# Two feed-forward blocks: one 512-column matmul for the high and low activation halves, and an evacuation in two parts

## The chip, the cores and the metric

The kernel runs on one core of one Trainium2 chip. The metric is the device time of one execution in microseconds; lower is better. The core has five engines with queues of their own: PE (TensorE, matmuls, with its weight loads shown as PEld), DVE (VectorE), ACT (ScalarE), POOL (GpSimd) and SP (SyncE, which here only issues DMAs). They meet through semaphores.

## The reference, cut to what matters

Two transformer-like blocks run one after the other on 256 tokens of width 1024, all in float32. Each ends in a feed-forward part of hidden width 2816, and only these two parts are touched:

```
# block 1 (conv_ffn), grid rows of 64 tokens
u, g = split(h @ up_w, 2)                 # (256,1024) @ (1024,5632)
g = g_left*w[0] + g*w[1] + g_right*w[2] + b   # within each row of 64 tokens
y = (silu(g) * u) @ down_w
# block 2
gate, up = split(hn @ w_gate_up, 2)
h = h + (silu(gate) * up) @ w_down
```

## The kernel before, in words

**Split precision.** Every large product is computed from halves. A weight or activation is rounded to `hi` (the engine's fp32r format), and `lo` is the remainder; the product is hi·hi + hi·lo + lo·hi, three matmuls (`mm3`, lines 1917 to 1922). Activations stand transposed (features on partitions, 256 tokens along the row) in `h_hi` and `h_lo`, each [128, 8, 256].

**Weights.** A weight group of 1 MB arrives by DMA in one of three slots of `raw`; ACT casts it to `w_hi` (`hi_ahead`, line 658), DVE subtracts to make `w_lo` (`lo_ahead`, line 1261), and PE then reads both. All three rings have three slots. ACT may cast group s once PE has used group s-3 (`group_used`); SP may load group s once DVE has finished group s-3 (`lo_ready`).

**Feature tiles.** In the stages `up` (22 groups) and `gate_up` (22 groups) one weight group is one tile: 8 slices k of 128 inputs by 256 output features, that is two runs f of 128 features. `feature_tiles` (line 1986) multiplies, for each f and k, three matmuls of 256 columns (tokens) each: 48 in a tile. One tile fills one PSUM bank of 512 columns (f = 0 in the first half, f = 1 in the second). The first tile in each pass of the loop takes another order (lines 1993 to 2009), 48 matmuls too, with waits for the activations.

**Pairs.** Tiles 2j and 2j+1 are a pair j (gate and up of the same features), 11 pairs, run as a hardware loop of three rounds of three pairs (u = 0, 1, 2) and two pairs behind it. `up` puts its pairs in banks (4,5), (0,1), (2,3), `gate_up` in (0,1), (2,3), (4,5). PE starts pair j once DVE has finished pair j-3 (`act_full`).

**Evacuation of `up`, pair j.** ACT (line 933): two Identity activations from PSUM (middle tap and bias) into `cv`, cast of weight group 2j+3, Silu of `cv`, cast of group 2j+4, cast of the product to `act_hi`. DVE (line 1604): four `scalar_tensor_tensor` (left and right tap, for each f) that read PSUM and add into `cv`, `w_lo` of group 2j+3, the product `cv` times the up tile from PSUM into `actf`, `w_lo` of group 2j+4, `act_lo`.

**Evacuation of `gate_up`, pair j.** ACT (line 1168): Silu straight from PSUM, the two weight casts, cast to `act2_hi`. DVE (line 1855): `w_lo` of group 2j+3, the product from PSUM, `w_lo` of 2j+4, `act2_lo`.

The `down` and `down2` products that follow use 512-column matmuls: the activations are the stationary operand and 512 weight columns move. `m_bcast` (line 2273) is the one fp32r matmul whose moving operand consists of two separate runs of 256 columns (`mw[:, :, d, :]`).

Of the kernel before, what the change touches and what calls it, by code (L numbers as in the profile page):

```python
# [14 lines left out]
F32R = mybir.dt.float32r  # L15
ALU = mybir.AluOpType
# [3 lines left out]
P = 128  # L20
# [31 lines left out]
NORM_BANKS = {"norm2": (6, 7, 2, 3), "norm3": (4, 5, 0, 1), "norm4": (4, 5, 6, 7),}  # L52
TOKEN_BANKS = (4, 5, 6, 3)
NEG = -1.0e30


def plan_groups(I):
# [74 lines left out]
def two_blocks(nc, I, out):  # L132
# [5 lines left out]
    with ExitStack() as ctx:  # L138
# [15 lines left out]
        }  # L154

        FAMILY["act_full"] = (("up", ROUND + PAIRS), ("gate_up", ROUND + PAIRS))
        for kind in ("conv_mid", "conv_done", "silu_ready", "act_hi_ready", "act_lo"):
# [23 lines left out]
        x = sb(ctx, "x", [P, TT, D])  # L181
        full = sb(ctx, "full", [P, KD, T])
        yg = full[:].rearrange("p k t -> p (k t)").rearrange("p (t n) -> p t n", t=TT)
        h_hi = sb(ctx, "h_hi", [P, KD, T], F32R)
        h_lo = sb(ctx, "h_lo", [P, KD, T], F32R)
        ident = sb(ctx, "ident", [P, P])
        s_le_t = sb(ctx, "s_le_t", [P, P])
        s_ge_t = sb(ctx, "s_ge_t", [P, P])
# [187 lines left out]

        def p_rows(n):
            return out[0, :, n * NB:(n + 1) * NB].rearrange("(t p) n -> p t n", p=P)

        def in_round(s, r):  # L380

# [263 lines left out]
        def _(act):  # L645
# [287 lines left out]
            def up_step(r, u):  # L933
                j = ROUND * r + u
                act.wait_ge(group_used, U0 + 2 * j + 1)
                act.wait_ge(S("act_full"), j + 1)
                for f in range(2):
                    k = 2 * j + f
                    act.activation(cv[:, u, f, :], ps[:, up_bank(u), f * T:(f + 1) * T], ACT.Identity,
                                   bias=pcol("conv_b", k), scale=pcol("conv_w", KF + k)).then_inc(S("conv_mid"), 1)  # L940
                hi_ahead(U0 + 3, r, u)
                act.wait_ge(S("conv_done"), 2 * j + 2)
                act.activation(cv[:, u], cv[:, u], ACT.Silu).then_inc(S("silu_ready"), 1)
                hi_ahead(U0 + 4, r, u)
                act.wait_ge(S("act_full"), ROUND + j + 1)
                act.copy(act_hi[:, bass.ds(2 * j, 2), :], actf[:, u]).then_inc(S("act_hi_ready"), 1)
# [280 lines left out]
        def _(dve):  # L1227
# [364 lines left out]

            post_norm("post1", "norm2", gp1, (2, 4), p_parts)
            dve.sem_inc(S("act_full"), ROUND)
            transposed("norm2", NORM_BANKS["norm2"], lambda k: mod2[:, KD + k:KD + k + 1], lambda k: mod2[:, k:k + 1])

            def half_of(bank):
# [5 lines left out]

            def up_step(r, u):
                j = ROUND * r + u
                for f in range(2):
                    k = 2 * j + f
                    dve.wait_ge(S("conv_mid"), 2 * j + 2)
# [5 lines left out]
                    dve.scalar_tensor_tensor(rows[:, :, :-1], src[:, :, 1:], pcol("conv_w", 2 * KF + k), rows[:, :, :-1],  # L1614
                                             ALU.mult, ALU.add).then_inc(S("conv_done"), 1)
                lo_ahead(U0 + 3, r, u)
                dve.wait_ge(S("silu_ready"), j + 1)
                dve.wait_ge(group_used, U0 + 2 * j + 2)
                dve.tensor_tensor(actf[:, u], cv[:, u], half_of(up_bank(u) + 1), ALU.mult).then_inc(S("act_full"), 1)
# [234 lines left out]

            def gate_up_step(r, u):
                j = ROUND * r + u
                lo_ahead(V0 + 3, r, u)
                dve.wait_ge(S("silu_ready"), PAIRS + j + 1)
                dve.wait_ge(group_used, V0 + 2 * j + 2)
                dve.tensor_tensor(actf2[:, u], sil[:, u], half_of(2 * u + 1), ALU.mult).then_inc(S("act_full"), 1)  # L1860
# [55 lines left out]
        def _(pe):  # L1916
# [69 lines left out]
            def feature_tiles(s, bank, r=0, ready=None, between=None):  # L1986


                s, r = in_round(s, r)
                pe.wait_ge(lo_ready, s + 1 + 2 * ROUND * r)  # L1990
                hi, lo = part_view(w_hi, s), part_view(w_lo, s)
                if ready is not None:
                    for f in range(2):
                        fs_ = slice(f * P, (f + 1) * P)
                        for k in range(KD):
                            if f == 0:
                                pe.wait_ge(S("hi"), base("hi", ready) + k + 1)
# [12 lines left out]
                for f in range(2):  # L2010
                    if f == 1 and between is not None:
                        between()
                    fs_ = slice(f * P, (f + 1) * P)
                    for k in range(KD):
                        ins = mm3(ps[:, bank, f * T:(f + 1) * T], (hi[:, k, fs_], lo[:, k, fs_]),
                                  (h_hi[:, k, :], h_lo[:, k, :]), k == 0, k == KD - 1)
                ins.then_inc(group_used, 1)

            def tile_turned(t):
# [351 lines left out]
            def ffn(name, norm, bank):  # L2371

                def step(r, u):
                    pe.wait_ge(S("act_full"), base("act_full", name) + ROUND * r + u + 1)
                    if name == "up" and u == 1:
                        pe.wait_ge(S("p_out"), TT)
                    for half in range(2):
                        feature_tiles(at[name][2 * u + half], bank(u) + half, r, norm if u == half == 0 else None)

                rounds(pe, step)  # L2380

            def second(name, first, hi, lo, banks, gate=None, middle=None, tail_groups=2):

                pe.wait_ge(S("act_full"), base("act_full", first) + PAIRS + ROUND - 2)
# [8 lines left out]
                gate_vector(3, 0)  # L2393

            transposed("norm2", lambda: p_product(0))
            ffn("up", "norm2", up_bank)
            second("down", "up", act_hi, act_lo, (2, 6), gate=gate2, tail_groups=3)


# [296 lines left out]
                att_out(2, t)  # L2696
                att_out(3, t)
            transposed("norm4")
            ffn("gate_up", "norm4", lambda u: 2 * u)
# [36 lines left out]
```

## Time and profile before

| what | value |
|---|---|
| median of 3 runs | 824.05 us (822.19 to 825.15) |
| profiled execution, its time | 822.81 us |
| its span | 821.0 us |
| PE busy share of the span | 96% |
| DVE / ACT busy share | 62% / 48% |
| granted PE clock, mean | 0.993 of full |

The span is the time from the first to the last instruction in the profile; the execution's own time is 1.8 us longer. The matmuls overlap each other, so a matmul's duration is a latency; how fast they follow each other is read from the start times.

### The profile page before, as it was taken

Reading aid. Unit: us, or ns where it says so; the run is one execution under the profiler, and the core shown is the slowest. Engines: PE = TensorE matmul, PEld = TensorE weight load, DVE = VectorE, ACT = ScalarE, POOL = GpSimd, SP = SyncE. Lnnn points to the kernel's source line nnn. Section 1 sums busy time; section 2 is a strip of 40 time slices with the busy share of each in tenths; the row PEclk is TensorE's granted clock in tenths of the full one; section 3 lists DMA queues with packets and bytes.
Section 4 is the critical chain, followed back from the end, with each engine's and each line's share of the span. In section 5 each row is a group of like instructions: output and inputs, shape, how many; then the busy total and the mean of one; then the engine's idle time right before and its main releaser. Section 6 shows DMA issues by size and latency. Waiting matters only on the chain. (4 is left out here: it accounts for less than half of the span.)

```text
span 821.0 us, 12736 instructions
## 1 busy us (share of the span) xinstructions
PE 786.1 (96%) x5175; PEld 701.5 (85%) x5175; DVE 511.3 (62%) x670; ACT 390.3 (48%) x538; POOL 92.7 (11%) x150
## 2 busy tenths in 40 slices
PE   4898999999999999999989999999999999999996
PEld 3677777777799999988789988988799999998884
DVE  1664789866685766667477785664464545454465
ACT  2623413444675565544366555456364443433264
POOL 4000221301100000000070313210100000000000
PEclk9999999999999999999999999999999999999998
DMA  9973577733276545569536342321465555546611
GB/s 308 361 242 132 200 265 263 263 103 127 92 231 205 165 163 185 203 226 317 175 95 192 103 154 75 110 75 58 148 229 165 195 187 170 191 145 203 221 62 52
DMA packets 107901, 144.85 MB, mean 176 GB/s; under 512 B 6343, under 2 KB 70352, under 8 KB 107856
## 3 DMA queue, kind: packets, MB, share of 16 engines
q1 hardware_dynamic: 100512, 137.38, 50.3%
q10 hardware_dynamic: 7280, 6.83, 2.7%
q8 instruction: 32, 0.52, 0.3%
q14 instruction: 13, 0.11, 0.0%
q0 software_dynamic: 64, 0.01, 0.0%
HBM read 142.10 MB, written 2.10 MB: 176 GB/s over the span
## 5 line engine op out<-in xcount | busy, mean ns | idle before, releaser
L1920 PE MATMUL ps<-h_hi,w_hi 128*128 128x256 f32 x720 | 204.5, 284 | 0.3 <-DVE w_lo L1257 0.3
L1921 PE MATMUL ps<-h_lo,w_hi 128*128 128x256 f32 x720 | 203.7, 283 | 0.0
L1922 PE MATMUL ps<-h_hi,w_lo 128*128 128x256 f32 x720 | 203.7, 283 | 0.0
L1257 DVE TENSOR_TENSOR w_lo<-raw,w_hi 128x2048 fp32r<-128x2048 f32 (+1 forms) x61 | 135.3, 2225 | 64.2 <-ACT w_hi L655 64.0
L655 ACT CAST w_hi<-raw 128x2048 fp32r<-128x2048 f32 (+1 forms) x61 | 112.9, 1852 | 79.1 <-PE ps L1922 60.1
L1265 DVE TENSOR_TENSOR w_lo<-raw,w_hi 128x2048 fp32r<-128x2048 f32 x44 | 100.8, 2290 | 60.8 <-ACT w_hi L663 60.8
L1920 PEld LDWEIGHTS ps<-h_hi,w_hi 128*128 128x128 f32 x720 | 138.2, 192 | 0.5 <-DVE w_lo L1257 0.5
L1921 PEld LDWEIGHTS ps<-h_lo,w_hi 128*128 128x128 f32 x720 | 138.2, 192 | 0.0
L1922 PEld LDWEIGHTS ps<-h_hi,w_lo 128*128 128x128 f32 x720 | 138.2, 192 | 0.0
L663 ACT CAST w_hi<-raw 128x2048 fp32r<-128x2048 f32 x44 | 83.5, 1899 | 50.6 <-PE ps L1922 50.5
L1920 PE MATMUL ps<-w_hi,act_hi 128*128 128x512 f32 x176 | 69.0, 392 | 0.0
L1921 PE MATMUL ps<-w_lo,act_hi 128*128 128x512 f32 x176 | 68.5, 389 | 0.0
L1922 PE MATMUL ps<-w_hi,act_lo 128*128 128x512 f32 x176 | 68.5, 389 | 0.0
L1920 PE MATMUL ps<-w_hi,h_hi 128*128 128x512 f32 x160 | 65.0, 406 | 3.2 <-DVE w_lo L1257 2.1
L1922 PE MATMUL ps<-w_hi,h_lo 128*128 128x512 f32 x160 | 63.1, 394 | 0.0
L1921 PE MATMUL ps<-w_lo,h_hi 128*128 128x512 f32 x160 | 63.0, 393 | 0.0
L1920 PEld LDWEIGHTS ps<-w_hi,h_hi 128*128 128x128 f32 x160 | 30.4, 190 | 12.1 <-issue 3.8
L1920 PEld LDWEIGHTS ps<-w_hi,act_hi 128*128 128x128 f32 x176 | 33.1, 188 | 7.0 <-issue 0.2
L1922 PEld LDWEIGHTS ps<-w_hi,act_lo 128*128 128x128 f32 x176 | 33.0, 188 | 7.0
L1921 PEld LDWEIGHTS ps<-w_lo,act_hi 128*128 128x128 f32 x176 | 33.1, 188 | 6.9 <-issue 0.2
L487 POOL TENSOR_SCALAR ss<-ss 128x1 f32<-128x1 f32 x14 | 5.5, 396 | 281.3 <-ACT junk L673 281.3
L1999 PE MATMUL ps<-h_hi,w_hi 128*128 128x256 f32 x144 | 37.0, 295 | 0.0
(399 smaller groups left out, 1308.2 us busy)
## 6 DMA issues: line engine op xcount, KB each, us to landing
raw<-in_ffn_up_w SPq DMA_DIRECT2D x22, 1024.0 KB, 5.1
raw<-in_w_gate_up SPq DMA_DIRECT2D x22, 1024.0 KB, 5.1
raw<-in_ada_w SPq DMA_DIRECT2D x16, 1024.0 KB, 5.2
raw<-in_w_in SPq DMA_DIRECT2D x14, 1024.0 KB, 5.3
raw<-in_m_in_w SPq DMA_DIRECT2D x11, 1024.0 KB, 5.1
raw<-in_ffn_down_w SPq DMA_DIRECT2D x10, 1024.0 KB, 5.2
raw<-in_w_down SPq DMA_DIRECT2D x10, 1024.0 KB, 5.1
raw<-in_m_out_w SPq DMA_DIRECT2D x4, 1024.0 KB, 5.2
```

Of the source, the lines that this page charges most:

```text
L487: link(pool.tensor_scalar(s, s, ss[:, c0 + TT:c0 + TT + 1], EPS, ALU.add, ALU.add))
L655: act.copy(part_view(w_hi, s), raw_view(split[s])).then_inc(hi_ready, 1)
L663: act.copy(part_view(w_hi, s), raw_view(split[s])).then_inc(hi_ready, 1)
L1257: dve.tensor_tensor(part_view(w_lo, s), raw_view(split[s]), part_view(w_hi, s).bitcast(F32), ALU.subtract).then_inc(lo_ready, 1)
L1265: dve.tensor_tensor(part_view(w_lo, s), raw_view(split[s]), part_view(w_hi, s).bitcast(F32), ALU.subtract).then_inc(lo_ready, 1)
L1920: pe.matmul(dst, l_hi, r_hi, start=first, stop=False)
L1921: pe.matmul(dst, l_hi, r_lo, start=False, stop=False)
L1922: return pe.matmul(dst, l_lo, r_hi, start=False, stop=last)
L1999: pe.matmul(dst, hi[:, k, fs_], h_hi[:, k, :], start=f == k == 0, stop=False)
```

## The change

In both feed-forward stages a tile takes two PSUM banks, one for each f: the first 256 columns of a bank collect what is multiplied with the high activations, the last 256 columns collect w_hi times the low activations. `h_hi` and `h_lo` become the two halves of one tensor `h_parts`, so that w_hi times both can be one matmul with 512 columns (two runs of 256). There are now three places of two banks, one tile each, in turn: (4,5), (2,3), (6,7) in `up` and (2,3), (4,5), (0,1) in `gate_up`. ACT copies the low half of a tile to memory, DVE adds the high half to it, and Silu, convolution and product work on these sums. The first tile of each loop pass keeps 256-column matmuls.

```diff
+WIDE_BANKS = {"up": (4, 2, 6), "gate_up": (2, 4, 0)}
+def wide_banks(name, u, half):
+    return WIDE_BANKS[name][(2 * u + half) % 3]
-        h_hi = sb(ctx, "h_hi", [P, KD, T], F32R)
-        h_lo = sb(ctx, "h_lo", [P, KD, T], F32R)
+        h_parts = sb(ctx, "h_parts", [P, 2, KD, T], F32R)
+        h_hi, h_lo = h_parts[:, 0], h_parts[:, 1]
+        def wide_halves(bank):
+            return ps[:, bank:bank + 2, 0:T], ps[:, bank:bank + 2, T:2 * T]
# ACT, up_step
                 act.wait_ge(S("act_full"), j + 1)
+                act.copy(cv[:, u], wide_halves(wide_banks("up", u, 0))[1]).then_inc(S("part_out"), 1)
+                act.wait_ge(S("gate_ready"), 4 + 4 * j + 1)
                 for f in range(2):
                     k = 2 * j + f
-                    act.activation(cv[:, u, f, :], ps[:, up_bank(u), f * T:(f + 1) * T], ACT.Identity, ...
+                    act.activation(cv[:, u, f, :], actf[:, u, f, :], ACT.Identity, ...
                 hi_ahead(U0 + 3, r, u)
-                act.wait_ge(S("conv_done"), 2 * j + 2)
+                act.wait_ge(S("gate_ready"), 4 + 4 * j + 3)
                 act.activation(cv[:, u], cv[:, u], ACT.Silu).then_inc(S("silu_ready"), 1)
+                act.wait_ge(group_used, U0 + 2 * j + 2)
+                act.copy(actf[:, u], wide_halves(wide_banks("up", u, 1))[1]).then_inc(S("part_out"), 1)
                 hi_ahead(U0 + 4, r, u)
# ACT, gate_up_step
-                act.activation(sil[:, u], ps[:, 2 * u, :].rearrange("p (f t) -> p f t", f=2), ACT.Silu)\
+                act.copy(sil[:, u], wide_halves(wide_banks("gate_up", u, 0))[1]).then_inc(S("part_out"), 1)
+                hi_ahead(V0 + 3, r, u)
+                act.wait_ge(S("gate_ready"), 4 + 4 * PAIRS + 2 * j + 1)
+                act.activation(sil[:, u], sil[:, u], ACT.Silu)\
                     .then_inc(S("silu_ready"), 1)
-                hi_ahead(V0 + 3, r, u)
+                act.wait_ge(group_used, V0 + 2 * j + 2)
+                act.copy(actf2[:, u], wide_halves(wide_banks("gate_up", u, 1))[1]).then_inc(S("part_out"), 1)
# DVE, up_step
+                dve.wait_ge(S("part_out"), 4 * j + 1)
+                dve.tensor_tensor(actf[:, u], wide_halves(wide_banks("up", u, 0))[0], cv[:, u], ALU.add)...
-                    src = ps[:, up_bank(u), f * T:(f + 1) * T].rearrange("p (r w) -> p r w", w=GRID_W)
+                    src = actf[:, u, f, :].rearrange("p (r w) -> p r w", w=GRID_W)
                 lo_ahead(U0 + 3, r, u)
+                dve.wait_ge(S("part_out"), 4 * j + 4)
+                dve.tensor_tensor(actf[:, u], wide_halves(wide_banks("up", u, 1))[0], actf[:, u], ALU.add)...
-                dve.tensor_tensor(actf[:, u], cv[:, u], half_of(up_bank(u) + 1), ALU.mult)...
+                dve.tensor_tensor(actf[:, u], actf[:, u], cv[:, u], ALU.mult)...
# DVE, gate_up_step: the same two additions around lo_ahead, the product from memory
# PE
+            def wide_tiles(s, bank, r, ready=None):
...
+                for f in range(2):
+                    w, both = slice(f * P, (f + 1) * P), ps[:, bank + f, :].rearrange("p (a t) -> p a t", a=2)
+                    pe.matmul(both, hi[:, 0, w], h_parts[:, :, 0, :], start=True, stop=False)
+                    pe.matmul(both[:, 0], lo[:, 0, w], h_hi[:, 0, :], start=False, stop=False)
+                    for k in range(1, KD):
+                        pe.matmul(both[:, 0], lo[:, k, w], h_hi[:, k, :], start=False, stop=False)
+                        ins = pe.matmul(both, hi[:, k, w], h_parts[:, :, k, :], start=False, stop=k == KD - 1)
-                    pe.wait_ge(S("act_full"), base("act_full", name) + ROUND * r + u + 1)
-                    if name == "up" and u == 1:
-                        pe.wait_ge(S("p_out"), TT)
-                    for half in range(2):
-                        feature_tiles(at[name][2 * u + half], bank(u) + half, r, norm if u == half == 0 else None)
+                    pe.wait_ge(S("act_full"), base("act_full", name) + j + 2)
+                    wide_tiles(at[name][2 * u], wide_banks(name, u, 0), r, norm if u == 0 else None)
+                    if name == "up":
+                        pe.wait_ge(S("gate_ready"), 4 * j + 1)
+                    else:
+                        pe.wait_ge(S("silu_ready"), PAIRS + j)
+                    wide_tiles(at[name][2 * u + 1], wide_banks(name, u, 1), r)
```

So PE starts tile 2j once pair j-2 is finished (before: j-3), and tile 2j+1 once DVE has added the gate tile of pair j-1 (in `gate_up`: once ACT has its Silu). `second` waits for one pair more than before.

## Rows read from the trace of the kernel before

**Rows 1.** Page, part 1: busy us (share of the span) xinstructions
```profile
PE 786.1 (96%) x5175; PEld 701.5 (85%) x5175; DVE 511.3 (62%) x670; ACT 390.3 (48%) x538; POOL 92.7 (11%) x150
```

**Rows 2.** Stages: window, length, busy PE, PEld, DVE, ACT, POOL, clock, DMA
```profile
229.00:350.00 121.00, 121.00 (x1009) 121.00 (x1009) 81.74 (x86) 69.63 (x70) 0.00 (x0) 1.00 0.60 195
604.00:727.00 123.00, 123.00 (x1027) 123.00 (x1026) 64.46 (x43) 50.46 (x42) 0.00 (x0) 1.00 0.57 188
```

**Rows 3.** Page, part 5: groups, busy us, mean ns | idle before
```profile
L1922 PE MATMUL ps<-h_hi,w_lo 128*128 128x256 f32 x720 | 203.7, 283 | 0.0
...
L1999 PE MATMUL ps<-h_hi,w_hi 128*128 128x256 f32 x144 | 37.0, 295 | 0.0
```

**Rows 4.** Timeline of PE, `up`: start us, duration us, line, form
```profile
228.76 0.38 PE L1920 MATMUL ps<-h_hi,w_hi 128*128 128x256 f32 x1 [0.25 <-DVE w_lo L1257]
...
349.69 0.28 PE L1922 MATMUL ps<-h_hi,w_lo 128*128 128x256 f32 x1
349.81 0.40 PE L1920 MATMUL ps<-w_hi,act_hi 128*128 128x512 f32 x1
```

**Rows 5.** Timeline of PE, `down`
```profile
352.33 0.39 PE L1922 MATMUL ps<-w_hi,act_lo 128*128 128x512 f32 x1
...
374.99 0.39 PE L1920 MATMUL ps<-w_hi,act_hi 128*128 128x512 f32 x1
```

**Rows 6.** Timeline of PE, gate weights of 32 columns
```profile
60.91 0.28 PE L2128 MATMUL ps<-h_hi,wg_parts 128*32 128x256 f32 x1
...
64.58 0.40 PE L2154 MATMUL ps<-w_hi,c_hi 128*128 128x512 f32 x1
```

**Rows 7.** Timeline of PE around L2273
```profile
141.81 0.73 PE L2273 MATMUL ps<-mw,sel 64*128 64x512 f32 x2
142.47 0.50 PE L1920 MATMUL ps<-w_hi,h_hi 128*128 128x512 f32 x1
142.81 0.39 PE L1921 MATMUL ps<-w_lo,h_hi 128*128 128x512 f32 x1
```

**Rows 8.** Timeline of DVE, `up`, one ordinary pair
```profile
241.94 0.48 DVE L1611 SCALAR_TENSOR_TENSOR cv<-ps,cols,cv 128x252 f32<-128x252 f32 x1 [1.37 <-ACT cv L939]
...
243.98 2.28 DVE L1265 TENSOR_TENSOR w_lo<-raw,w_hi 128x2048 fp32r<-128x2048 f32 x1
246.33 0.69 DVE L1619 TENSOR_TENSOR actf<-cv,ps 128x512 f32<-128x512 f32 x1
248.26 2.29 DVE L1265 TENSOR_TENSOR w_lo<-raw,w_hi 128x2048 fp32r<-128x2048 f32 x1 [1.24 <-ACT w_hi L663]
250.47 0.68 DVE L1269 TENSOR_TENSOR act_lo<-actf,act_hi 128x512 f32 x1
```

**Rows 9.** Timeline of ACT, the same pair
```profile
240.78 1.02 ACT L939 ACTIVATE cv<-ps,cols 128x256 f32<-128x256 f32 x2 [2.61 <-PE ps L1922]
241.70 1.90 ACT L663 CAST w_hi<-raw 128x2048 fp32r<-128x2048 f32 x1
244.10 0.63 ACT L943 ACTIVATE cv<-cv 128x512 f32<-128x512 f32 x1 [0.50 <-DVE cv L1614]
```

**Rows 10.** Timeline of ACT, start of `up`
```profile
227.56 1.15 ACT L697 COPY p_out<-ps 128x512 f32<-128x512 f32 x2
...
229.62 1.28 ACT L939 ACT_TABLE_LOAD   x1 [0.91 <-ACT p_out L697]
...
233.74 1.28 ACT L943 ACT_TABLE_LOAD   x1
```

**Rows 11.** Timeline of DVE, start of `up`
```profile
226.42 4.49 DVE L1257 TENSOR_TENSOR w_lo<-raw,w_hi 128x2048 fp32r<-128x2048 f32 x2
...
234.13 2.28 DVE L1265 TENSOR_TENSOR w_lo<-raw,w_hi 128x2048 fp32r<-128x2048 f32 x1
```

**Rows 12.** Timeline of DVE, `gate_up`, one pair
```profile
620.41 2.29 DVE L1265 TENSOR_TENSOR w_lo<-raw,w_hi 128x2048 fp32r<-128x2048 f32 x1 [3.43 <-ACT w_hi L663]
623.67 0.69 DVE L1860 TENSOR_TENSOR actf<-sil,ps 128x512 f32<-128x512 f32 x1 [0.97 <-PE ps L1922]
```

**Rows 13.** Page, part 6: DMA issues, KB each, us to landing
```profile
raw<-in_ffn_up_w SPq DMA_DIRECT2D x22, 1024.0 KB, 5.1
```

More of the change, by code:

```diff
@@ L156, in two_blocks @@
         FAMILY["act_full"] = (("up", ROUND + PAIRS), ("gate_up", ROUND + PAIRS))
-        for kind in ("conv_mid", "conv_done", "silu_ready", "act_hi_ready", "act_lo"):
+        for kind in ("part_out", "gate_ready", "silu_ready", "act_hi_ready", "act_lo"):
             FAMILY[kind] = (("up", PAIRS), ("gate_up", PAIRS))
@@ L936, in up_step @@
                 act.wait_ge(S("act_full"), j + 1)
+                act.copy(cv[:, u], wide_halves(wide_banks("up", u, 0))[1]).then_inc(S("part_out"), 1)
+                act.wait_ge(S("gate_ready"), 4 + 4 * j + 1)
                 for f in range(2):
                     k = 2 * j + f
-                    act.activation(cv[:, u, f, :], ps[:, up_bank(u), f * T:(f + 1) * T], ACT.Identity,
-                                   bias=pcol("conv_b", k), scale=pcol("conv_w", KF + k)).then_inc(S("conv_mid"), 1)
+                    act.activation(cv[:, u, f, :], actf[:, u, f, :], ACT.Identity,
+                                   bias=pcol("conv_b", k), scale=pcol("conv_w", KF + k)).then_inc(S("part_out"), 1)
                 hi_ahead(U0 + 3, r, u)
-                act.wait_ge(S("conv_done"), 2 * j + 2)
+                act.wait_ge(S("gate_ready"), 4 + 4 * j + 3)
                 act.activation(cv[:, u], cv[:, u], ACT.Silu).then_inc(S("silu_ready"), 1)
+                act.wait_ge(group_used, U0 + 2 * j + 2)
+                act.copy(actf[:, u], wide_halves(wide_banks("up", u, 1))[1]).then_inc(S("part_out"), 1)
                 hi_ahead(U0 + 4, r, u)
@@ L1594, in _ @@
             dve.sem_inc(S("act_full"), ROUND)
+            dve.sem_inc(S("gate_ready"), 4)
             transposed("norm2", NORM_BANKS["norm2"], lambda k: mod2[:, KD + k:KD + k + 1], lambda k: mod2[:, k:k + 1])
@@ L1605, in up_step @@
                 j = ROUND * r + u
+                dve.wait_ge(S("part_out"), 4 * j + 1)
+                dve.tensor_tensor(actf[:, u], wide_halves(wide_banks("up", u, 0))[0], cv[:, u], ALU.add).then_inc(S("gate_ready"), 1)
                 for f in range(2):
                     k = 2 * j + f
-                    dve.wait_ge(S("conv_mid"), 2 * j + 2)
+                    dve.wait_ge(S("part_out"), 4 * j + 3)
                     rows = cv[:, u, f, :].rearrange("p (r w) -> p r w", w=GRID_W)
-                    src = ps[:, up_bank(u), f * T:(f + 1) * T].rearrange("p (r w) -> p r w", w=GRID_W)
+                    src = actf[:, u, f, :].rearrange("p (r w) -> p r w", w=GRID_W)
                     dve.scalar_tensor_tensor(rows[:, :, 1:], src[:, :, :-1], pcol("conv_w", k), rows[:, :, 1:],
@@ L1614, in up_step @@
                     dve.scalar_tensor_tensor(rows[:, :, :-1], src[:, :, 1:], pcol("conv_w", 2 * KF + k), rows[:, :, :-1],
-                                             ALU.mult, ALU.add).then_inc(S("conv_done"), 1)
+                                             ALU.mult, ALU.add).then_inc(S("gate_ready"), 1)
                 lo_ahead(U0 + 3, r, u)
+                dve.wait_ge(S("part_out"), 4 * j + 4)
+                dve.tensor_tensor(actf[:, u], wide_halves(wide_banks("up", u, 1))[0], actf[:, u], ALU.add).then_inc(S("gate_ready"), 1)
+                dve.wait_ge(S("gate_ready"), 4 + 4 * j + 4)
                 dve.wait_ge(S("silu_ready"), j + 1)
-                dve.wait_ge(group_used, U0 + 2 * j + 2)
-                dve.tensor_tensor(actf[:, u], cv[:, u], half_of(up_bank(u) + 1), ALU.mult).then_inc(S("act_full"), 1)
+                dve.tensor_tensor(actf[:, u], actf[:, u], cv[:, u], ALU.mult).then_inc(S("act_full"), 1)
                 lo_ahead(U0 + 4, r, u)
@@ L1856, in gate_up_step @@
                 j = ROUND * r + u
+                dve.wait_ge(S("part_out"), 4 * PAIRS + 2 * j + 1)
+                dve.tensor_tensor(sil[:, u], wide_halves(wide_banks("gate_up", u, 0))[0], sil[:, u], ALU.add).then_inc(S("gate_ready"), 1)
                 lo_ahead(V0 + 3, r, u)
+                dve.wait_ge(S("part_out"), 4 * PAIRS + 2 * j + 2)
+                dve.tensor_tensor(actf2[:, u], wide_halves(wide_banks("gate_up", u, 1))[0], actf2[:, u], ALU.add).then_inc(S("gate_ready"), 1)
+                dve.wait_ge(S("gate_ready"), 4 + 4 * PAIRS + 2 * j + 2)
                 dve.wait_ge(S("silu_ready"), PAIRS + j + 1)
-                dve.wait_ge(group_used, V0 + 2 * j + 2)
-                dve.tensor_tensor(actf2[:, u], sil[:, u], half_of(2 * u + 1), ALU.mult).then_inc(S("act_full"), 1)
+                dve.tensor_tensor(actf2[:, u], actf2[:, u], sil[:, u], ALU.mult).then_inc(S("act_full"), 1)
                 lo_ahead(V0 + 4, r, u)
@@ L2016, in feature_tiles @@
                                   (h_hi[:, k, :], h_lo[:, k, :]), k == 0, k == KD - 1)
+                ins.then_inc(group_used, 1)
+            def wide_tiles(s, bank, r, ready=None):
+                s, r = in_round(s, r)
+                pe.wait_ge(lo_ready, s + 1 + 2 * ROUND * r)
+                hi, lo = part_view(w_hi, s), part_view(w_lo, s)
+                if ready is not None:
+                    for f in range(2):
+                        for k in range(KD):
+                            if f == 0:
+                                pe.wait_ge(S("hi"), base("hi", ready) + k + 1)
+                            dst, w = ps[:, bank + f, 0:T], slice(f * P, (f + 1) * P)
+                            pe.matmul(dst, hi[:, k, w], h_hi[:, k, :], start=k == 0, stop=False)
+                            pe.matmul(dst, lo[:, k, w], h_hi[:, k, :], start=False, stop=False)
+                    for f in range(2):
+                        for k in range(KD):
+                            if f == 0:
+                                pe.wait_ge(S("hT"), base("hT", ready) + k + 1)
+                            ins = pe.matmul(ps[:, bank + f, T:2 * T], hi[:, k, f * P:(f + 1) * P], h_lo[:, k, :], start=False,
+                                            stop=k == KD - 1)
+                    ins.then_inc(group_used, 1)
+                    return
+                for f in range(2):
+                    w, both = slice(f * P, (f + 1) * P), ps[:, bank + f, :].rearrange("p (a t) -> p a t", a=2)
[4 more added lines that the diff above has]
+                        ins = pe.matmul(both, hi[:, k, w], h_parts[:, :, k, :], start=False, stop=k == KD - 1)
                 ins.then_inc(group_used, 1)
@@ L2369, in _, with wide_products @@
             token_block(at["mix_out"][1], [(*X0, 4), (*X1, 5)], tail="t0_done")
-            def ffn(name, norm, bank):
+            def wide_products(name, norm):
                 def step(r, u):
-                    pe.wait_ge(S("act_full"), base("act_full", name) + ROUND * r + u + 1)
-                    if name == "up" and u == 1:
-                        pe.wait_ge(S("p_out"), TT)
-                    for half in range(2):
-                        feature_tiles(at[name][2 * u + half], bank(u) + half, r, norm if u == half == 0 else None)
+                    j = ROUND * r + u
+                    pe.wait_ge(S("act_full"), base("act_full", name) + j + 2)
[5 more added lines that the diff above has]
+                    wide_tiles(at[name][2 * u + 1], wide_banks(name, u, 1), r)
                 rounds(pe, step)
             def second(name, first, hi, lo, banks, gate=None, middle=None, tail_groups=2):
-                pe.wait_ge(S("act_full"), base("act_full", first) + PAIRS + ROUND - 2)
+                pe.wait_ge(S("act_full"), base("act_full", first) + PAIRS + ROUND - 1)
                 for n in range(2):
@@ L2395, in _ @@
             transposed("norm2", lambda: p_product(0))
-            ffn("up", "norm2", up_bank)
+            wide_products("up", "norm2")
             second("down", "up", act_hi, act_lo, (2, 6), gate=gate2, tail_groups=3)
@@ L2698, in _ @@
             transposed("norm4")
-            ffn("gate_up", "norm4", lambda u: 2 * u)
+            wide_products("gate_up", "norm4")
             second("down2", "gate_up", act2_hi, act2_lo, (4, 6), middle=lambda: tile_turned(0))
```

## The prediction

> **What bounds the kernel now.** I read the page's busy shares first, then the stages, then the start times of PE's matmuls, then the timelines of DVE and ACT inside one pair. PE is busy 96% of the span [rows 1], and in the two stages that the change touches 100%: 121.0 of 121.0 us and 123.0 of 123.0 us, at full granted clock, with DVE at 68% and 52% and ACT at 58% and 41% [rows 2]. A busy PE is not yet PE at its fastest, since durations overlap, so the start times decide. In `up` the first matmul of the second tile starts at 228.76 and the first of `down` at 349.81 [rows 4]: 21 tiles x 48 = 1008 matmuls in 121.05 us, 0.1201 us each, with no gap that the waits show. At 2.4 GHz (clock 1.00) 256 columns take 0.1067 us, so 0.0134 us of each matmul is not columns. In `down`, 100 matmuls of 512 columns lie between 352.33 and 374.99 [rows 5]: 0.2266 us each, of which 0.2133 are columns and 0.0133 are not. The fixed part is the same in both widths. PE is bound by its own stream: columns plus 0.0134 us for each matmul.
>
> **The change part by part.**
>
> *PE.* For each f and k, three matmuls of 256 columns (3 x 0.1201 = 0.3603 us) become one of 512 and one of 256 (0.2266 + 0.1201 = 0.3467 us). The columns stay: 768 before and after. What goes is one fixed part, 0.0136 us. A tile has 16 such triples. Not all tiles get it: the 144 instances of L1999 [rows 3] are 16 each in 9 tiles, 8 of them in the feed-forward stages (first tile of each of four loop passes, twice; the ninth is in another stage) and these keep 48 matmuls. That leaves 44 - 8 = 36 tiles, 576 triples: 576 x 0.0136 = 7.8 us, half in each stage.
>
> No row shows 512 and 256 columns in alternation, or this moving operand at speed, so I bound the pair. From below: with weights of only 32 columns a 256-column matmul takes (64.58 - 60.91)/32 = 0.1147 us [rows 6], so at most 0.0054 us of each fixed part hangs on the weight load. If the change hid that too, in both matmuls, the pair took 0.3359 us and the gain were 576 x 0.0244 = 14.1 us. From above: the one fp32r matmul that moves two runs of 256 columns takes 142.47 - 141.81 = 0.66 us for two, 0.33 us each [rows 7]. At that price the pair takes 0.45 us and the change costs 576 x (0.45 - 0.36) = +52 us. I take 0.3467, near the lower end, because the matmul behind them, with one contiguous run, also takes 0.34 us (142.47 to 142.81, same rows): the 0.33 belongs to the place (weights of 64 partitions, a change of format, a wait) and not to the two runs.
>
> The Trainium skill (TensorE: Matmul & The Clock Gate, Back-to-back issue gap) gives N/2.4 + 2.5 ns from one warm matmul to the next, 109.2 ns for 256 columns. The trace has 120.1. By the page a triple would save 2.5 ns, 1.4 us in all; by the rows 7.8. The rows decide, since they are this kernel's own stream of loads and matmuls.
>
> *PE's waits.* Six places of one bank become three of two, so a place comes round after three tiles. Tile 2j now waits for the product of pair j-2, which has two tiles, 11.1 us, from the end of tile 2j-3 (its pair's second). Tile 2j+1 waits for the addition of tile 2j-2, with 11.1 us too. Behind a waiting PE instruction the whole matmul stream is queued, so lateness here costs its full length. Before, the product was done 0.7 us after its tile (246.33 + 0.69, the tile having ended at 228.76 + 3 x 5.76 + 0.28 = 246.3) [rows 4, 8]. After, a copy (1.15 us for two, some 0.65 alone [rows 10]) and an addition (0.69, as L1619, which reads PSUM and memory too [rows 8]) come first, about 2.2 us in all, 3.5 where DVE is late. Both waits are met with 7 us to spare and cost nothing. The wait for `p_out` that goes had no time in it.
>
> *DVE in `up`.* This is the tightest. I lay out an ordinary pair from T0, the end of tile 2j, tiles at 5.55 us: ACT copy 0.05 to 0.70, DVE addition 0.80 to 1.49, ACT's two Identities 1.55 to 2.57 (1.02) [rows 9], four taps 2.70 to 4.74 (2.04, 241.94 to 243.98), `w_lo` of group 2j+3 to 6.95 (2.21 from start to start, 248.26 to 250.47) [rows 8], second addition to 7.6, product to 8.2, `w_lo` of 2j+4 to 10.4, `act_lo` to 11.0. The next pair's addition is due at 11.9. So DVE has 0.9 us over; when late, it goes round in 10.2 us and gains 0.9 us a pair on PE's 11.1. Where the loop begins a pass, two table loads of 1.28 us [rows 10] lie in this chain; the first costs 1.28, the second some 0.5, and that pair takes 12.0 us. Three pairs then need 12.0 + 2 x 10.2 = 32.4 of PE's 33.4 us. DVE keeps pace, with 1 us in each pass.
>
> *Who waits for DVE.* Tile 2j+3 needs its `w_lo` at T0 + 11.1 and has it at 7.0, in a first pair of a pass at 8.2. The worst place is the start: DVE is busy with weights until 230.9 [rows 11] while the first tile is done at 228.8, so the addition begins 2.1 us late, and `w_lo` of the fourth tile, now done at 236.4 (234.13 + 2.28), is done at about 238.4. PE comes to that tile at 228.76 + 2 x 5.55 = 239.9. Margin 1.5 us: no stall. SP's loads wait for `w_lo` and start up to 2 us later; a load lands after 5.1 us [rows 13], and ACT wants it 11 us after the slot is free. `act_lo` of the last pair is 2 us later but is read by the last `down` group, 27 us on. So all work added on ACT (two copies a pair) and DVE (two additions) is hidden; with the cover gone it would be 1.4 us for each of 11 pairs on DVE in `up`, 15 us.
>
> *DVE in `gate_up`.* From 620.41 to the product at 623.67 there is a pause of 0.97 us, and 3.43 us before it [rows 12]; the two additions, 1.4 us, fit.
>
> *Sum.* 0 + 0 - 7.8 us: span 821.0 - 7.8 = 813.2, the execution's own time 822.81 - 7.8 = 815.0. The median of the runs shown is 1.2 us above that execution; on it the sum gives 816.2. What follows each stage starts with PE's last matmul, so the gain is not given back. I forecast 816 us, own range 813 to 819.
>
> **The rivals.**
>
> A, slower: the two-run moving operand streams more slowly. It decides from 0.2402 us for the 512-column matmul (twice 0.1201) and costs up to 52 us, a time of 876, if all 576 take 0.33 [rows 7]. Against it: the contiguous matmul behind has the same spacing. 7%.
>
> B, DVE becomes the bound of `up`: if the additions, which read halves of two banks, take twice 0.69 us, a pair takes 11.6 and a first pair 13.4 us, three pairs 36.6 against 33.4; over 11 pairs 11.8 us, less some 3 us of reserve, is +9 us in `up` against -7.8 in all: about 825, no change. For it: 1 us of margin a pass. Against: L1619 reads 512 columns of PSUM at 0.69 [rows 8]. 9%.
>
> C, the fixed part is not one per matmul but one per 256 columns, once widths alternate: a triple then costs what it did, 0.36 us, and nothing is gained but nothing lost, 823 to 824, within 0.3%. Against: 0.2266 us in rows 5, where all are wide. 6%, of which I give 1% to a fixed part that is really so small (0.0025 us) that the change saves 576 x 0.0025 = 1.4 us, a time of 822.6; rows 4 speak against it. That last value is what the Trainium skill's formula in the section named above gives.
>
> D, more than forecast: the weight load of the 256-column matmul hides wholly behind the 512 columns before it: up to 14.1 us, 810. For it: rows 6. 11%.
>
> **How the numbers follow.** The forecast has 67%. The range reaches from rival D's end, with spread of the runs below it, to where B and C begin: 808 to 823. What a measurement here can tell from no change is 0.3%, 2.5 us: faster is below 821.6. Forecast and D give 78%, with 1% from a mild B: 0.79 faster. Same: C and most of B, 0.12. Slower: A and the rest, 0.09.
>
> **What would show it.** Right: PE starts in an ordinary `up` tile that alternate 0.227 and 0.120 us, a tile in 5.55 us instead of 5.76, `up` and `gate_up` each 3.9 us shorter, no PE wait above 0.3 us there, clock 1.00. Wrong: a 512-column spacing over 0.24 us (A or C), or PE idle before a tile, released by an addition, a product or `w_lo` (B). A pair below 0.34 us is D.

## Result: 6.8 us of 824 faster

| | before | after |
|---|---|---|
| median of 4 runs | 824.11 us (822.19 to 825.15) | 817.29 us (816.16 to 818.08) |
| profiled execution, its time | 822.81 us | 817.6 us |
| its span | 821.0 us | 815.9 us |

The ratio is 0.9926, interval [0.9907, 0.9945]: between 4.5 and 7.7 us gained, clear of no change but far below 2%. The forecast was 816, with 7.8 us gained.

The page's busy shares after, which answer to [rows 1]:

```profile
PE 780.6 (96%) x4599; PEld 669.7 (82%) x4599; DVE 540.0 (66%) x714; ACT 414.7 (51%) x582; POOL 92.5 (11%) x150
```

PE has 5175 - 4599 = 576 matmuls fewer, the 576 triples of the prediction. It is as busy as before, and DVE and ACT have more work. The two stages, each from its first matmul to the first of the `down` product behind it (window, length, busy us and instructions of PE, PEld, DVE, ACT, POOL, clock, DMA share, GB/s). Before:

```profile
221.41:349.81 128.40, 128.15 (x1060) 127.15 (x1059) 89.19 (x99) 76.92 (x83) 0.00 (x0) 1.00 0.56 184
599.99:727.15 127.16, 127.16 (x1059) 126.96 (x1058) 68.47 (x51) 54.23 (x49) 0.00 (x0) 1.00 0.57 190
```

After:

```profile
222.50:347.88 125.38, 125.10 (x771) 111.15 (x770) 100.98 (x120) 89.42 (x104) 0.00 (x0) 1.00 0.58 189
597.90:721.99 124.09, 124.09 (x771) 110.95 (x770) 82.95 (x72) 65.01 (x70) 0.00 (x0) 1.00 0.59 195
```

`up` is 3.02 us shorter and `gate_up` 3.07, 6.09 in all; half each, as forecast, but not 7.8. The rest of the span hardly moves: from the end of `up` to the start of `gate_up` 250.18 us before and 250.02 after, from the end of `gate_up` to the end of the span 93.85 and 93.91. Only the stretch ahead of `up`, whose instructions the change leaves as they were, is 1.09 us longer in this execution (222.50 against 221.41), and that is why the two spans differ by 5.1 and not by 6.1 us. In other profiles below that stretch ends anywhere from 220.75 to 225.21, so differences of 1 or 2 us between spans say nothing of an edit behind it. I compare stage lengths throughout.

PE's timeline after, in one tile of `up` (start us, duration us), which answers to [rows 4]:

```profile
241.17 0.39 PE L2070 MATMUL ps<-h_parts,w_hi 128*128 128x512 f32 x1
241.40 0.28 PE L2071 MATMUL ps<-h_parts,w_lo 128*128 128x256 f32 x1
241.51 0.28 PE L2073 MATMUL ps<-h_parts,w_lo 128*128 128x256 f32 x1
241.63 0.40 PE L2074 MATMUL ps<-h_parts,w_hi 128*128 128x512 f32 x1
241.87 0.28 PE L2073 MATMUL ps<-h_parts,w_lo 128*128 128x256 f32 x1
...
243.99 0.40 PE L2070 MATMUL ps<-h_parts,w_hi 128*128 128x512 f32 x1
...
246.76 0.39 PE L2070 MATMUL ps<-h_parts,w_hi 128*128 128x512 f32 x1
```

A wide matmul is followed after 0.23 to 0.24 us, a narrow one after 0.11 to 0.12. The tile takes 246.76 - 241.17 = 5.59 us, where it took 5.76. Over the 576 pairs of both stages the means are 0.2338 and 0.1159, together 0.3497 us; forecast were 0.3467. The tile's two halves, f = 0 and f = 1, are not alike: 2.82 us to 243.99, then 2.77. Experiment 9 comes back to this.

The only PE wait in `up` is the one that was there before, for the weights of the second tile:

```profile
PE ps L2070 <- DVE w_lo L1276: 0.3, 1, 0.3
```

DVE's timeline from one pair's first addition to the next one's, which answers to [rows 8]:

```profile
243.37 0.68 DVE L1627 TENSOR_TENSOR actf<-ps,cv 128x512 f32<-128x512 f32 x1
245.49 0.48 DVE L1633 SCALAR_TENSOR_TENSOR cv<-actf,cols,cv 128x252 f32<-128x252 f32 x1 [1.43 <-ACT cv L952]
...
247.54 2.28 DVE L1284 TENSOR_TENSOR w_lo<-raw,w_hi 128x2048 fp32r<-128x2048 f32 x1
249.74 0.68 DVE L1640 TENSOR_TENSOR actf<-ps,actf 128x512 f32<-128x512 f32 x1
250.55 0.69 DVE L1643 TENSOR_TENSOR actf<-actf,cv 128x512 f32<-128x512 f32 x1
251.16 2.28 DVE L1284 TENSOR_TENSOR w_lo<-raw,w_hi 128x2048 fp32r<-128x2048 f32 x1
253.36 0.68 DVE L1288 TENSOR_TENSOR act_lo<-actf,act_hi 128x512 f32 x1
253.96 0.68 DVE L1627 TENSOR_TENSOR actf<-ps,cv 128x512 f32<-128x512 f32 x1
```

The additions, which read half of two banks, take 0.68 us, no more than L1619 in [rows 8]. DVE, late here, goes round in 10.59 us against PE's 11.19 for two tiles.

### The profile page after: what moved, and what is told of

Its sections match the earlier page's. It is cut to its first block and busy times, and to the rows that moved or that the text cites. A ratio compares the mean times of both kernels' runs of the same rounds, so it can differ in the third digit from the quotient of the medians.

```text
span 815.9 us, 11773 instructions
## 1 busy us (share of the span) xinstructions
PE 780.6 (96%) x4599; PEld 669.7 (82%) x4599; DVE 540.0 (66%) x714; ACT 414.7 (51%) x582; POOL 92.5 (11%) x150
## 5 line engine op out<-in xcount | busy, mean ns | idle before, releaser
L2074 PE MATMUL ps<-h_parts,w_hi 128*128 128x512 f32 x504 | 179.6, 396 | 0.0
L2073 PE MATMUL ps<-h_parts,w_lo 128*128 128x256 f32 x504 | 140.5, 279 | 0.0
L2074 PEld LDWEIGHTS ps<-h_parts,w_hi 128*128 128x128 f32 x504 | 94.6, 188 | 19.5
L2073 PEld LDWEIGHTS ps<-h_parts,w_lo 128*128 128x128 f32 x504 | 95.0, 188 | 3.3
L1948 PE MATMUL ps<-w_hi,h_parts 128*128 128x512 f32 x160 | 64.9, 406 | 3.2 <-DVE w_lo L1276 2.1
L1949 PE MATMUL ps<-w_lo,h_parts 128*128 128x512 f32 x160 | 63.1, 394 | 0.0
L1950 PE MATMUL ps<-w_hi,h_parts 128*128 128x512 f32 x160 | 63.0, 394 | 0.0
L1948 PE MATMUL ps<-h_parts,w_hi 128*128 128x256 f32 x144 | 41.4, 288 | 0.0
L1949 PE MATMUL ps<-h_parts,w_hi 128*128 128x256 f32 x144 | 40.7, 283 | 0.0
L1950 PE MATMUL ps<-h_parts,w_lo 128*128 128x256 f32 x144 | 40.7, 283 | 0.0
L1948 PEld LDWEIGHTS ps<-w_hi,h_parts 128*128 128x128 f32 x160 | 30.3, 190 | 12.3 <-issue 4.0
```

What stands on the lines that cost most here:

```text
L1948: pe.matmul(dst, l_hi, r_hi, start=first, stop=False)
L1949: pe.matmul(dst, l_hi, r_lo, start=False, stop=False)
L1950: return pe.matmul(dst, l_lo, r_hi, start=False, stop=last)
L2073: pe.matmul(both[:, 0], lo[:, k, w], h_hi[:, k, :], start=False, stop=False)
L2074: ins = pe.matmul(both, hi[:, k, w], h_parts[:, :, k, :], start=False, stop=k == KD - 1)
```

## Experiments

The times of the kernel before that ran beside these are 823.0 to 823.5 us. Diffs are against the changed kernel.

**1. One run instead of two.** Is it the two runs of the moving operand that cost the extra 3 ns a pair?

```diff
-        h_parts = sb(ctx, "h_parts", [P, 2, KD, T], F32R)
-        h_hi, h_lo = h_parts[:, 0], h_parts[:, 1]
+        h_parts = sb(ctx, "h_parts", [P, KD, 2, T], F32R)
+        h_hi, h_lo = h_parts[:, :, 0, :], h_parts[:, :, 1, :]
...
-                        ins = pe.matmul(both, hi[:, k, w], h_parts[:, :, k, :], start=False, stop=k == KD - 1)
+                        ins = pe.matmul(both, hi[:, k, w], h_parts[:, k], start=False, stop=k == KD - 1)
```

> Layout of h_parts changed to [128, 8, 2, 256], so that the 512 columns of each wide matmul are one run; nothing else. After the change the wide matmul took 0.2338 us to the next start and the narrow one 0.1160, 0.3497 a pair, where 0.2266 + 0.1201 = 0.3467 was forecast. Theory R (the two runs of the moving operand cost the extra 7 ns): the wide one falls to 0.2266, the pair to 0.343 or 0.347, the time by 1.5 to 4 us below the changed kernel (813 to 815). Theory W (the extra lies in the alternation of widths): pair stays at 0.3497, time 817. Theory P (it lies in the order of weights and banks, whatever the operand): the same 817.

Measured: 817.3 us (816.55 to 819.72), ratio 0.9928. `up` takes 125.38 us, to the hundredth what it takes in the changed kernel. The timeline of this kernel:

```profile
241.18 0.28 PE L2073 MATMUL ps<-h_parts,w_lo 128*128 128x256 f32 x1
241.30 0.40 PE L2074 MATMUL ps<-h_parts,w_hi 128*128 128x512 f32 x1
241.54 0.28 PE L2073 MATMUL ps<-h_parts,w_lo 128*128 128x256 f32 x1
```

0.24 and 0.12 again, in the mean 0.2338 and 0.1159 as before. Theory R is out, and with it rival A: two runs cost nothing here. The 0.33 us of L2273 [rows 7], the upper bound of my range of costs, is then not the price of two runs; which part of its place it came from no run shows.

**2. Wide ones together.** Is it the alternation of widths?

```diff
-                    pe.matmul(both, hi[:, 0, w], h_parts[:, :, 0, :], start=True, stop=False)
-                    pe.matmul(both[:, 0], lo[:, 0, w], h_hi[:, 0, :], start=False, stop=False)
-                    for k in range(1, KD):
-                        pe.matmul(both[:, 0], lo[:, k, w], h_hi[:, k, :], start=False, stop=False)
-                        ins = pe.matmul(both, hi[:, k, w], h_parts[:, :, k, :], start=False, stop=k == KD - 1)
+                    for k in range(KD):
+                        pe.matmul(both, hi[:, k, w], h_parts[:, :, k, :], start=k == 0, stop=False)
+                    for k in range(KD):
+                        ins = pe.matmul(both[:, 0], lo[:, k, w], h_hi[:, k, :], start=False, stop=k == KD - 1)
```

> In each bank the eight wide matmuls first, then the eight narrow ones; two runs kept. Theory R: wide stays at 0.234, narrow to narrow 0.1201, sum 0.354 a pair, time 576 x 0.0044 = 2.5 us above the changed kernel (820). Theory W: wide to wide 0.2266, narrow 0.1201, sum 0.3467, time 576 x 0.003 = 1.7 us below (815.5).

Measured: 817.66 us (816.58 to 820.03); `up` 125.31 us, `gate_up` 124.03. Its timeline (a row now holds eight matmuls):

```profile
238.25 2.00 PE L2071 MATMUL ps<-h_parts,w_hi 128*128 128x512 f32 x8
240.09 1.11 PE L2073 MATMUL ps<-h_parts,w_lo 128*128 128x256 f32 x8
241.04 2.00 PE L2071 MATMUL ps<-h_parts,w_hi 128*128 128x512 f32 x8
```

Eight pairs take 241.04 - 238.25 = 2.79 us, 0.349 a pair: (240.09 - 238.25)/8 = 0.230 and 0.95/8 = 0.119. Neither theory's number: each stage is only 0.07 us shorter, 0.2 ns a pair, so about a tenth of the 3 ns comes back. Inside a group of eight wide ones the first six take 0.232 us each (241.04 to 242.43), the last two 0.227.

**3. Evacuation alone.** Does the added work of ACT and DVE cost or give anything by itself?

```diff
...
-                        ins = pe.matmul(both, hi[:, k, w], h_parts[:, :, k, :], start=False, stop=k == KD - 1)
+                        pe.matmul(both[:, 0], hi[:, k, w], h_hi[:, k, :], start=k == 0, stop=False)
+                        pe.matmul(both[:, 1], hi[:, k, w], h_lo[:, k, :], start=False, stop=False)
+                        ins = pe.matmul(both[:, 0], lo[:, k, w], h_hi[:, k, :], start=False, stop=k == KD - 1)
```

> The banks, places and evacuation in two parts of the changed kernel, but three 256-column matmuls again in every tile, as before. My theory (all added work of ACT and DVE is hidden, the gain is PE's stream alone): the time of before, 824, with a tile in 5.76 us and no new wait of PE. Rival (part of what was gained or lost lies in the evacuation or in the places): over 826 or under 822.

Measured: 823.12 us against 823.04, ratio 0.9999 [0.9984, 1.0015]. The two stages:

```profile
221.11:349.52 128.41, 128.14 (x1060) 127.15 (x1058) 101.34 (x120) 89.57 (x104) 0.00 (x0) 1.00 0.57 184
601.24:728.39 127.15, 127.15 (x1059) 126.95 (x1058) 82.98 (x72) 64.94 (x70) 0.00 (x0) 1.00 0.58 190
```

128.41 and 127.15 us are the lengths of before to 0.01 us, with 12 us more busy time on DVE and on ACT in `up`. PE's only wait in `up` is again the 0.3 us for the second tile's `w_lo`. So the places and the evacuation are hidden whole, and the gain is PE's stream alone.

**4. Both 1 and 2.** The matmuls of experiment 2 on the layout of experiment 1; this cut is against experiment 2.

```diff
-                        pe.matmul(both, hi[:, k, w], h_parts[:, :, k, :], start=k == 0, stop=False)
+                        pe.matmul(both, hi[:, k, w], h_parts[:, k], start=k == 0, stop=False)
```

> Grouped as the second, contiguous as the first. Theory R and theory W both: wide 0.2266, narrow 0.1201, a pair 0.3467, time 815.5. If it stays at 0.350 or more a pair, neither names the cause, and the width alone does not set the spacing.

Measured: 817.46 us; `up` 125.31, `gate_up` 124.03, the same as experiment 2, so a pair is at 0.349 and not at the 0.3467 that both theories gave. Neither the runs nor the alternation one by one names the cause; the next one asks what 512 columns cost here without any change of width.

**5. Only wide ones.** Low weights times both halves as well.

```diff
...
-                        pe.matmul(both[:, 0], lo[:, k, w], h_hi[:, k, :], start=False, stop=False)
-                        ins = pe.matmul(both, hi[:, k, w], h_parts[:, :, k, :], start=False, stop=k == KD - 1)
+                    for k in range(KD):
+                        pe.matmul(both, hi[:, k, w], h_parts[:, :, k, :], start=k == 0, stop=False)
+                        ins = pe.matmul(both, lo[:, k, w], h_parts[:, :, k, :], start=False, stop=k == KD - 1)
```

> In the 36 wide tiles the low weights too are multiplied with both halves, so every matmul there has 512 columns (the output gains the lo x lo term, which neither the kernel nor the reference needs). It gives the steady spacing of 512-column matmuls in these stages, without any change of width. In `down` it is 0.2266 us. Theory S (the spacing of a 512-column matmul is the same everywhere, and the 0.2338 beside 0.1160 is only how alternation shares the sum): 0.2266, time 817 + 576 x (0.4532 - 0.3497) = 877. Theory T (in these stages each matmul has a little more than the 0.0134 us, whatever its width): 0.228 to 0.231, time 879 to 882. Theory R2 (a 512-column matmul here takes 0.234 by itself): 885.

Measured: 878.21 us (2 runs). Of its timeline, the first and the last of 30 matmuls:

```profile
239.78 0.39 PE L2071 MATMUL ps<-h_parts,w_hi 128*128 128x512 f32 x1
...
246.35 0.39 PE L2072 MATMUL ps<-h_parts,w_lo 128*128 128x512 f32 x1
```

6.57/29 = 0.2266 us, exactly the spacing of `down` [rows 5]. Theory S holds: in a stream of its own width a wide matmul costs the same here as there.

**6 and 7. How much has DVE to spare?** One, then three more additions in each pair of `up`, ahead of the first one.

```diff
+                for i in range(1):        # 3 in the seventh
+                    dve.tensor_tensor(spare[:], wide_halves(wide_banks("up", u, 0))[0], cv[:, u], ALU.add).then_inc(S("conv_left"), 1)
+                    dve.wait_ge(S("conv_left"), 3 * j + i + 1)    # 5 * j in the seventh
                 dve.tensor_tensor(actf[:, u], wide_halves(wide_banks("up", u, 0))[0], cv[:, u], ALU.add)...
...
```

> One more 128x512 addition in each pair of `up` on DVE, ahead of the first one, in its chain (0.8 us with its own wait). DVE goes round in 10.6 us per ordinary pair against PE's 11.2. Theory D (DVE has under 1 us a pair to spare, and a reserve of 2 to 3 us before PE stands still): three pairs then need 32.0 + 2.4 = 34.4 us of PE's 33.7, 0.7 us too many a pass, 2.6 us in all, swallowed by the reserve: 817 to 818.5, DVE's idle time in `up` under 1 us. Rival (PE has much more slack than the timelines show, or none): no change in DVE's idle time, or over 821.

> Three more such additions a pair (2.4 us). Theory D: three pairs need 39.2 us of 33.7; 3.7 passes x 5.5 = 20 us less the reserve of 2 to 3, so 834 to 836, with PE waiting for w_lo or for additions in every pair. Rival (slack hidden elsewhere, other engines overlap better): under 826.

Measured: with one 818.9 us (817.69 to 820.62), `up` 125.53 us against 125.38. The median of the four lies 0.4 us above the forecast; the profiled execution, the longest of them, came to `up` at 225.21, 2.7 us late, and the stage is the measure. DVE's timeline there, two starts of a pair's chain:

```profile
258.14 0.68 DVE L1629 TENSOR_TENSOR spare<-ps,cv 128x512 f32<-128x512 f32 x1
269.46 0.68 DVE L1629 TENSOR_TENSOR spare<-ps,cv 128x512 f32<-128x512 f32 x1
```

A pair takes 11.32 us on DVE, already more than PE's 11.19: DVE falls behind a little with each pair and the stage is over before it costs more than 0.15 us. DVE's waits for ACT's first copy, 4.5 us over `up` in the changed kernel, are down to 0.5.

With three 834.39 us (831.87 to 837.4), `up` 139.63 us. PE's waits there:

```profile
PE ps L2074 <- DVE w_lo L1285: 11.7, 9, 1.6
PE ps L2074 <- DVE w_lo L1277: 0.3, 1, 0.3
```

and DVE's timeline, one round:

```profile
309.73 2.14 DVE L1629 TENSOR_TENSOR spare<-ps,cv 128x512 f32<-128x512 f32 x3
311.90 0.69 DVE L1631 TENSOR_TENSOR actf<-ps,cv 128x512 f32<-128x512 f32 x1
...
322.72 2.13 DVE L1629 TENSOR_TENSOR spare<-ps,cv 128x512 f32<-128x512 f32 x3
```

This round, the first of a pass, takes 12.99 us where the changed kernel has 10.83 (265.87 to 276.70); the others take 12.78 for 10.59. Each is longer than PE's 11.19, and that paces PE. From the first pair's first addition to the last pair's DVE takes 127.8 us instead of 110.6 (232.61 to 360.45, 232.52 to 343.11), 17.2 more, of which 14.25 appear in the stage: PE lives on a reserve of 3 us before it stands still. Theory D holds, with the reserve at the upper end of what it said. The changed `up` stage with its 11 pairs has room for one such addition in a pair, not for three; two were not tried, and by the 11.32 us of a round even one would cost time in a stage of many more pairs.

**8. The first tile too.** 34 matmuls instead of 48 in the first tile of each loop pass.

```diff
...
+                            pe.matmul(ps[:, bank + f, 0:T], lo[:, k, f * P:(f + 1) * P], h_hi[:, k, :], start=k == 0, stop=False)
+                            if k == 0:
+                                pe.matmul(ps[:, bank + f, 0:T], hi[:, 0, f * P:(f + 1) * P], h_hi[:, 0, :], start=False, stop=False)
...
+                            dst, act = (both, h_parts[:, :, k, :]) if k else (both[:, 1], h_lo[:, 0, :])
+                            ins = pe.matmul(dst, hi[:, k, f * P:(f + 1) * P], act, start=False, stop=k == KD - 1)
```

> The first tile of each loop pass uses wide matmuls too: first all low weights times the high half (and high times high for k = 0), then high weights times both halves for k = 1 to 7, two narrow ones for k = 0; 34 matmuls instead of 48. Theory: the six tiles that are first of a later pass gain 14 x 0.0106 = 0.15 us each, 0.9 us; the two tiles at the start of a stage, which wait for the low half to be made, come out even within 0.5 us: 816.3 against 817.2. Rival: the wide ones behind the waits lose at the start what the others gain, 817.2 or more.

Measured: 816.76 us (815.38 to 820.31). The stages:

```profile
222.01:346.97 124.96, 124.61 (x715) 108.22 (x714) 101.00 (x120) 89.39 (x104) 0.00 (x0) 1.00 0.57 189
598.74:722.99 124.25, 124.25 (x716) 108.18 (x715) 83.04 (x72) 64.99 (x70) 0.00 (x0) 1.00 0.59 195
```

`up` gains 0.42 us, `gate_up` loses 0.16. The first tile of `gate_up` takes 6.77 us instead of 6.20, and 0.57 us of loss there are more than the 0.14 that each of the three later tiles brings. With this order the part ahead of the low half has only 18 matmuls to put between its waits for slices of the high half, of which four take 0.36 us each, and is over after 3.31 us instead of 4.28; the part behind it takes 3.46 instead of 1.92. The sum, 0.26 us, is neither theory's, and in the medians it doesn't show.

**9. Only wide ones, grouped.** In experiment 5 each slice of the activations moved twice in a row, in experiment 2 never. Does a new slice with each matmul cost the 3 ns?

```diff
...
+                    for k in range(KD):
+                        pe.matmul(both, hi[:, k, w], h_parts[:, :, k, :], start=k == 0, stop=False)
+                    for k in range(KD):
+                        ins = pe.matmul(both, lo[:, k, w], h_parts[:, :, k, :], start=False, stop=k == KD - 1)
```

> All matmuls of the 36 tiles wide, as in the fifth experiment (lo x lo added), but in each bank first the eight with high weights, then the eight with low ones, so that each matmul moves another slice than the one before it. In the fifth, where each slice moved twice in a row, the spacing was 0.2268 us; in the second, with eight wide ones in a row on eight slices and narrow ones behind, 0.2301. Theory V (a new moving slice with each matmul costs the 3 ns): 0.230, time 878 + 1152 x 0.003 = 882. Theory W2 (a stream that changes its width carries the 3 ns, whatever moves): 0.2268, time 878.

Measured: 876.69 us (2 runs). Its timeline:

```profile
240.53 1.98 PE L2071 MATMUL ps<-h_parts,w_hi 128*128 128x512 f32 x8
242.34 1.98 PE L2073 MATMUL ps<-h_parts,w_lo 128*128 128x512 f32 x8
...
249.59 1.98 PE L2073 MATMUL ps<-h_parts,w_lo 128*128 128x512 f32 x8
```

40 matmuls in 249.59 - 240.53 = 9.06 us, 0.2265 each. Theory V is out. Of W2 the first part holds: in a stream of one width the spacing is 0.2266 or 0.1201, whatever moves. The second part, that a change of width carries the 3 ns, holds only in the mean (3.0 ns a pair, 2.5 if grouped by eight). In the changed kernel's timeline above, the first half of the tile takes 243.99 - 241.17 = 2.82 us, 0.352 a pair, the second 246.76 - 243.99 = 2.77, 0.347, which is the forecast sum, and the widths alternate in both alike. All 36 tiles do so: 2.81 to 2.82 us and 2.78, but for the very first half (2.93), which holds a wait. So nearly the whole excess stands in the first halves, 5 ns a pair, and the change of width alone is not its cause.

Nor do the weight columns or the bank of the first half name it. In experiment 7, behind a short standstill of PE, the two halves change parts:

```profile
241.33 0.50 PE L2074 MATMUL ps<-h_parts,w_hi 128*128 128x512 f32 x1
244.21 0.39 PE L2074 MATMUL ps<-h_parts,w_hi 128*128 128x512 f32 x1
247.03 0.40 PE L2074 MATMUL ps<-h_parts,w_hi 128*128 128x512 f32 x1
```

The first half takes 2.88 us, of which 0.10 is the longer time behind its first matmul (0.335 us, as in the other tiles behind a wait), so 2.78 without it; the second takes 2.82. The tile at 292.87, behind a wait of 1.57 us, does the same; most tiles behind a wait do not. So the same instructions run in either time, by how the stream comes to them. What it is in the stream that decides is open.

**10. The best parts together.** The order of experiment 2 everywhere, the first tile of experiment 8 in `up` alone.

```diff
-                if ready is not None:
+                if ready == "norm4":       # the narrow first tile, for gate_up; else that of experiment 8
```

> The best parts together: wide matmuls grouped ahead of the narrow ones in every bank, and the wide first tile in `up` alone (in the eighth experiment `up` took 0.42 us less and `gate_up` 0.16 us more). By the stages: `up` 125.38 - 0.42 - 0.07, `gate_up` 124.09 - 0.06, so 0.55 us below the changed kernel, 816.7; a rival, that the two edits take the same nanoseconds, 817.1 or more. Both lie within the spread of the runs, so the stages in the trace decide, not the median.

Measured: 817.78 us (815.18 to 819.78), `up` 124.83 us, `gate_up` 124.05: 248.88 against 249.47 of the changed kernel, 0.59 us shorter, as the stages had promised, with a profiled span of 814.1. The medians of 6 and 4 runs don't show it. By the stages it is the shortest of all; that it is faster in time than the changed kernel is not shown.

## Why the prediction was right, and where its size was off

- **What bounds.** PE's own stream at full clock: right. Experiment 3 adds 12 us of work to DVE and to ACT and leaves both stages as they were to 0.01 us; experiments 5 and 9 add columns and the time follows (60 us in the two stages, 576 x (0.4532 - 0.3497) = 60).
- **The terms of a pair.** The count was exact: 576 matmuls gone, 36 tiles, 8 left alone. The size was not. I added the spacing of a stream of 512 (0.2266) and of one of 256 (0.1201), 0.3467, and named this as something that no row shows. It is 0.3497. The saving of a triple is 0.0106 us instead of 0.0136, and 576 x 0.0106 = 6.1 us is what the stages show, for 7.8 forecast. Experiments 5 and 9 say which half of the assumption failed: each spacing is right by itself, the sum is not, in half of the places where widths mix. Why PE takes 5 ns a pair more in the first halves is not settled: experiment 1 excludes the layout of the moving operand, 9 the change of the moving slice, the second halves the change of width as such, 3, 5 and 9 the load from DVE and ACT (beside the same work pure streams keep 0.120 and 0.2266). My sign against rivals A and C, no 512-column spacing over 0.24 us, holds for the mean of 0.234; single ones reach 0.241.
- **The fixed part.** By the Trainium skill's formula (TensorE: Matmul & The Clock Gate, Back-to-back issue gap) the change would have brought 1.4 us. The same section calls the formula that of an isolated matmul and says that a stream of weight loads and matmuls is spaced by both, which the prediction left out; it gives 131 ns for 512 columns in such a stream, where this trace has 226.6. The trace gave the better forecast, 7.8, and the runs 6.1: the fixed part of these fp32r matmuls is 13 ns and not 2.5, and the rival that rested on 2.5 is out.
- **The size of the time.** That 817.3 came so near to 816 is in part luck. The stages gained 6.1 us and the medians differ by 6.8; experiment 1, with the same stages, lies 5.7 us below the kernel before that ran beside it.
- **The waits of PE.** None new, as forecast. The fourth tile's `w_lo`, the place I called the worst, is ready at 239.0 (236.71 + 2.29) and PE comes to it at 241.17: margin 2.2 us, 1.5 forecast.
- **DVE in `up`.** I laid its round out at 10.2 us and it is 10.59: 0.12 us more from the addition to the Identity activations, 0.10 more from there to the taps (Identity from memory takes 1.09 for two and not 1.02), 0.16 more from the second addition to the product. The first pair of a pass, which I put at 12.0 because of the table loads, takes 10.83 (265.87 to 276.70). Three late pairs then need 10.83 + 2 x 10.59 = 32.0 us of the 33.7 that PE takes for a pass: a margin of 1.7, where I had 1. The two errors went opposite ways. Experiments 6 and 7 show how thin it is: one more addition a pair lifts DVE's round above PE's, three cost 14 us. Rival B, two more such times a pair, was near and did not come, since the additions take 0.68 us each.
- **`gate_up`.** The same gain, 3.07 us to 3.02, with DVE busy 67% of the stage, as forecast.
- **The rivals.** A is excluded by experiment 1, B by PE's waits, C by the gain itself (a triple that cost what it did would have left the stages as in experiment 3), D by the pair of 0.3497, which lies above and not below the sum.

## What to carry to other kernels

Where PE is the bound and never waits, count what each matmul costs beyond its columns from the start times, not from durations, and multiply it by the matmuls that a wider form takes away; if the new stream mixes widths, allow a few ns a pair more than the sum of the two pure spacings (here 0 to 5). A wider form that needs more PSUM can pay with work on other engines, but lay out one round of the busiest of them against PE's beforehand: here 0.6 us in 11.2 were left. Compare the stages and not the spans where an edit is worth less than the stretches around it vary.

## What the runs showed of the hardware that was not expected

- Mixed widths: 0.2338 + 0.1159 = 0.3497 us alternating, 0.349 grouped by eight, against 0.2266 + 0.1201 = 0.3467 in pure streams; the wide one gets longer and the narrow one shorter. Alternating, the excess comes and goes by half tiles: 2.82 us for eight pairs in the one, 2.78 in the other.
- A moving operand in two runs of 256 columns, 8 KB apart, streams as fast as one run: the same 125.38 us for the whole stage.
- The profiled start of `up`, behind code that all kernels share, varied from 220.75 to 225.21 us.
